# Gate and up projections: a second level of the seven-product scheme in six of ten weight slots, and one order of products

## The chip, the cores and the metric

The kernel runs on one core of one Trainium2 chip. The metric is device time in microseconds; the median of three runs of the kernel before is 2923.05 us.

## What is computed

The program is two different two-layer transformer stacks, one behind the other. The change lies in the feed-forward part of the second stack's two layers:

```python
def swiglu_ffn(u, w_gate_up, w_down):
    g, up = jnp.split(u @ w_gate_up, 2, axis=-1)
    return (jax.nn.silu(g) * up) @ w_down
```

`u` is 512 tokens by 1024 features, float32. `w_gate_up` has 2 x 2816 columns, `w_down` 2816 rows. What comes before it in each layer (mixing, attention over a memory) and the whole first stack with its experts are untouched.

## The kernel before

**Slots.** The gate and up weights come in 11 slots of 512 columns: two tiles of 128 gate columns and the two tiles of 128 up columns that belong to them, for all 1024 rows (2 MB). Two slots are in SBUF at a time; SyncE loads slot n + 2 when slot n has been read. Slot 0 is multiplied plainly. Slots 1 to 10 go by the Winograd form of Strassen's scheme: with the rows of the weights cut into a low and a high half, gate and up as the other cut, and the 512 tokens cut into two halves, the 2 x 2 by 2 x 2 block product is made with seven block products in place of eight.

**The seven products.** `a11`, `a12` are the low and high rows of gate, `a21`, `a22` those of up. VectorE forms `s1` to `s4` from them for every slot (`form_sums`, lines 2526 to 2531, four operations of 1024 columns) and `t1` to `t4` once a layer from the tokens. TensorE makes `P1 = a11 b11`, `P2 = a12 b21`, `P6 = s2 t2`, `P7 = s3 t3`, `P5 = s1 t1`, `P4 = a22 t4`, `P3 = s4 b22` (all products are issued at line 2551, `block_product`). A slot is worked as two chunks of 128 gate columns; each product is then four matmuls of 128 x 128 weights by 256 tokens, and each float32 matmul is two MATMUL records, each with a weight load. ScalarE copies P1, P7 and P5 from PSUM into small buffers (lines 3109 to 3112) and applies SiLU (3114, 3116), VectorE adds the others to them (3119, 3121, 3129, 3130) and multiplies gate by up (3133, 3136), and GpSimd makes the three sums that two corners share (3140, 3142, 3144). Each chunk uses four PSUM banks, the next one the other four.

**What sets the order.** Each engine runs its own fixed list; semaphores tie them together. Counters with the places of the steps in those lists say what to wait for (`g_full`, `g_act`, `g_dve`, `g_pool`, `g_sums`). VectorE forms the sums for the next slot in the middle of the second chunk's work. After the gate slots come eight slots of the down projection, which use the same scheme and the same banks.

Of the kernel before, what the change touches and what calls it, by code (L numbers as in the profile page):

```python
# [5 lines left out]
P = 128  # L6
# [73 lines left out]
def program(nc, a):  # L80
# [5 lines left out]
    with ctx:  # L86
# [2395 lines left out]
        quarters = [view(wk, i * 256, 256) for i in range(8)] + [view(rows, i * 256, 256) for i in range(4)]  # L2482
        feat_diff = [view(big, i * 1024, KC // 2, 256) for i in range(4)]
        w_sum = [[view(big, 4096 * (1 + b) + i * 1024, KC // 2, 256) for i in range(4)] for b in range(2)]
# [4 lines left out]
        FAST = {"mix": 10, "query": 2, "gate": FC - 2, "down": 4}  # L2489
        UP_FULL, SILU = {k: 7 for k in STAGES}, {"mix": 3, "query": 3, "gate": 5, "down": 5}  # L2490
        HIDDEN, ADDED = {"mix": 4, "query": 4, "gate": 6, "down": 4}, {k: 3 for k in STAGES}
        SUMS = {"mix": 6, "query": 2, "gate": FC // 2, "down": DOWN_SLOTS}

        def stage_base(per, halves, l, stage):
            each = [per[k] * FAST[k] // halves for k in STAGES]
            return l * sum(each) + sum(each[:STAGES.index(stage)])

        def g_full(stage, l, n, i):
            return LAYERS * PAIRS + stage_base(UP_FULL, 2, l, stage) + 7 * (n // 2) + 4 * (n % 2) + i + 1

        def g_act(stage, l, n, i):
            return LAYERS * PAIRS + stage_base(SILU, 1, l, stage) + SILU[stage] * n + i + 1

        def g_dve(stage, l, n, i):
            return LAYERS * PAIRS + stage_base(HIDDEN, 1, l, stage) + HIDDEN[stage] * n + i + 1

        def g_pool(stage, l, n, i):
            return stage_base(ADDED, 1, l, stage) + 3 * n + i + 1

        def g_sums(stage, l, b):  # L2510
            return l * sum(SUMS.values()) + sum(SUMS[k] for k in STAGES[:STAGES.index(stage)]) + b + 1

# [29 lines left out]

        def weight_sums(dve, n, w, b):

            dve.wait_ge(w_loaded[n % 2], 16 * (n // 2 + 1))
            sums(dve, w, w_sum[b % 2])
# [527 lines left out]
        P1_P2, P6_, P7_P5, P4_P3 = range(4)  # L3074
        P1_READ, P7_READ, P5_READ, LOW_SILU, HIGH_SILU = range(5)
        LOW_GATE, U2_READY, HIGH_GATE, LOW_UP, LOW_DONE, HIGH_DONE = range(6)
        U3_READY, HIGH_UP, U4_READY = range(3)

        def fast_chunk(name, eng, l, k, w, block_end, after_u2=None):

            b, i = divmod(k, 2)
            n = k - 2
            cols = slice(i * P, (i + 1) * P)
            p1_, p7_, p5_, u2, low, high = quarters[6 * (n % 2):6 * (n % 2) + 6]
            first, second = split_banks(fast_banks[l][n % 2])
            if name == "pe":
                gate, up = w[:, :, cols], w[:, :, 256 + i * P:256 + (i + 1) * P]
                s1, s2, s3, s4 = (v[:, :, cols] for v in w_sum[b % 2])
                t1, t2, t3, t4 = feat_diff
                lo, hi = LOW_K, HIGH_K  # L3090

                if k >= 4:
                    eng.wait_ge(hidden_ready, g_dve("gate", l, n - 2, LOW_UP))
# [8 lines left out]
            if name == "act":  # L3102
                if k == 2:
                    eng.wait_ge(bank_read_dve, reads_of[up_at[l, 1]]["dve"])
                if n >= 2:
                    eng.wait_ge(outer_added, g_pool("gate", l, n - 2, U4_READY))
                    eng.wait_ge(hidden_ready, g_dve("gate", l, n - 2, HIGH_DONE))
                eng.wait_ge(up_full, g_full("gate", l, n, P1_P2))
                A.activation(p1_, first[0], ACT.Copy).then_inc(silu_ready, 1)
                eng.wait_ge(up_full, g_full("gate", l, n, P7_P5))  # L3110
                A.activation(p7_, first[2], ACT.Copy).then_inc(silu_ready, 1)
                A.activation(p5_, second[2], ACT.Copy).then_inc(silu_ready, 1)
                eng.wait_ge(hidden_ready, g_dve("gate", l, n, LOW_GATE))
                A.activation(low, low, ACT.Silu).then_inc(silu_ready, 1)
                eng.wait_ge(hidden_ready, g_dve("gate", l, n, HIGH_GATE))
                A.activation(high, high, ACT.Silu).then_inc(silu_ready, 1)
            if name == "dve":
                eng.wait_ge(silu_ready, g_act("gate", l, n, P1_READ))
                V.tensor_tensor(low, p1_, second[0], ALU.add).then_inc(hidden_ready, 1)
                eng.wait_ge(up_full, g_full("gate", l, n, P6_))  # L3120
                V.tensor_tensor(u2, p1_, first[1], ALU.add).then_inc(hidden_ready, 1)
                if after_u2 is not None:
                    after_u2()
                if i:
                    eng.wait_ge(bank_full, block_end + 1)
                else:
                    eng.wait_ge(up_full, g_full("gate", l, n, P4_P3))
                eng.wait_ge(outer_added, g_pool("gate", l, n, U4_READY))
                V.tensor_tensor(high, p5_, second[3], ALU.add).then_inc(hidden_ready, 1)
                V.tensor_tensor(hidden[:, k, LO], p7_, first[3], ALU.add).then_inc(hidden_ready, 1)  # L3130
                eng.wait_ge(silu_ready, g_act("gate", l, n, LOW_SILU))
                eng.drain()
                V.tensor_tensor(hidden[:, k, LO], hidden[:, k, LO], low, ALU.mult).then_inc(hidden_ready, 1)
                eng.wait_ge(outer_added, g_pool("gate", l, n, HIGH_UP))
                eng.wait_ge(silu_ready, g_act("gate", l, n, HIGH_SILU))
                V.tensor_tensor(hidden[:, k, HI], hidden[:, k, HI], high, ALU.mult).then_inc(hidden_ready, 1)
# [12 lines left out]
        def gate_up(name, eng, l):  # L3149
# [19 lines left out]
            for blk in range(FC // 2):  # L3169
                n = take(name, "ring")  # L3170
                w = ring_slot(n, KC, 512)
                if name == "pe":
                    eng.wait_ge(w_loaded[n % 2], 16 * (n // 2 + 1))
                if name == "pe" and blk == 0:
                    first, second, banks = slice(0, 2 * P), slice(2 * P, 4 * P), []
                    feat_ready(eng, 1)
                    for i in range(2):
# [4 lines left out]
                        if i == 0:  # L3182
                            turn_x(name, eng, TT - 1)
# [653 lines left out]
```

## Time and profile before

| | us |
|---|---|
| median of three runs (2922.53 to 2923.17) | 2923.05 |
| span of the profiled execution | 2921.3 |
| TensorE busy, of the span | 2810.8 |
| VectorE busy | 1110.9 |
| ScalarE busy | 663.0 |
| GpSimd busy | 512.2 |

The busy time of an engine is the union of its records. Matmul records overlap, since a matmul is pipelined behind the one before it; the distance between their starts is what one costs in a long row of them. PE is TensorE, PEld its weight loads, DVE VectorE, ACT ScalarE, POOL GpSimd. An operation on VectorE that has no `drain` before it starts a little before the end of the one ahead; after a `drain` it starts a little behind that end.

### The profile page before, as it was taken

What the parts mean: (1) busy time and instruction counts of PE and PEld (TensorE: products, weight loads), DVE (VectorE), ACT (ScalarE), POOL (GpSimd) and SP (SyncE); (2) the same over time, 40 slices, a digit from 0 to 9 for tenths busy, and PEclk for the clock granted to TensorE, in tenths of its full rate; (3) what the DMA queues carried; (4) which work ended last, traced back from release to release, by engine and by line L of the source; (5) the groups of instructions that cost most, each with busy time, mean ns of one, the idle gap of its engine ahead of it and who ended that gap; (6) DMA issues with size and microseconds to landing.
All of it is one profiled execution on the core that took longest, in us unless ns stands there. A gap on an engine that the chain in (4) does not pass through costs nothing.

```text
span 2921.3 us, 32166 instructions
## 1 busy us (share of the span) xinstructions
PE 2810.8 (96%) x12444; PEld 1896.7 (65%) x12444; DVE 1110.9 (38%) x2252; ACT 663.0 (23%) x1512; POOL 512.2 (18%) x785
## 2 busy tenths in 40 slices
PE   8999999899999998999999999999999999999998
PEld 4565543355656432686565688888686575788887
DVE  4543311154433111445432333354446332333354
ACT  3333110033331100105422211101206412211100
POOL 3101111131111111113200022201114410122201
PEclk9999999999999999999999999999999999999999
DMA  3206799831067998420020222222220111122222
GB/s 135 75 29 252 292 425 423 363 127 56 30 259 305 424 425 359 175 87 30 30 87 29 87 87 87 72 80 94 87 87 30 49 67 47 69 87 87 72 90 84
DMA packets 106579, 422.13 MB, mean 145 GB/s; under 512 B 10096, under 2 KB 14320, under 8 KB 91440
## 3 DMA queue, kind: packets, MB, share of 16 engines
q1 hardware_dynamic: 93104, 387.01, 34.1%
q0 software_dynamic: 12736, 30.84, 2.8%
q8 instruction: 104, 1.70, 0.2%
q10 hardware_dynamic: 576, 2.10, 0.2%
q14 instruction: 59, 0.48, 0.1%
HBM read 408.63 MB, written 27.26 MB: 149 GB/s over the span
## 4 chain that ended last, share of the span: by engine, by line
PE 77%; issue 9%; DMA 7%; DVE 2%; ACT 2%; POOL 1%; POOLq 1%; DVEq 0%; SPq 0%; ACTq 0%
PE ps L2551 35%; PE ps L1773 6%; DMA ring_feat<-in_w 5%; PE ps L431 5%; PE ps L2792 4%; PE ps L2819 4%; PE ps L1112 3%; PE ps L1814 3%; PE ps L2693 2%; PE ps L2839 2%; PE ps L3153 2%; PE ps L1339 2%; PE ps L2283 1%; PE ps L2070 1%; PE ps L2265 1%
## 5 line engine op out<-in xcount | busy, mean ns | idle before, releaser
L431 PE MATMUL ps<-ring_feat 128*128 128x512 f32 (+2 forms) x704 | 274.9, 545 | 4.9 <-DMA ring_feat<-in_w_lat 2.8
L2551 PE MATMUL ps<-ring_feat 128*128 128x256 f32 x1216 | 277.0, 379 | 1.6 <-ACT big L287 1.6
L2551 PE MATMUL ps<-big 128*128 128x256 f32 x1200 | 268.1, 379 | 0.0
L2551 PEld LDWEIGHTS ps<-ring_feat 128*128 128x128 f32 x1216 | 230.9, 190 | 34.5 <-issue 3.3
L2551 PEld LDWEIGHTS ps<-big 128*128 128x128 f32 x1200 | 228.0, 190 | 31.0
L431 PEld LDWEIGHTS ps<-ring_feat 128*128 128x128 f32 x704 | 132.7, 191 | 130.6 <-issue 93.6
L2551 PE MATMUL ps<-tmp 128*128 128x256 f32 x576 | 128.6, 379 | 0.0
L2551 PE MATMUL ps<-ring_feat,tmp 128*128 128x256 f32 x544 | 126.6, 379 | 0.0
L2551 PEld LDWEIGHTS ps<-tmp 128*128 128x128 f32 x576 | 109.3, 190 | 14.8
L2792 PE MATMUL ps<-ring_feat 128*128 128x512 f32 x256 | 113.9, 596 | 5.0 <-ACT ring_feat L3052 2.7
L1112 PE MATMUL ps<-ring_feat 128*128 128x512 f32 x256 | 113.7, 595 | 0.0
L2551 PEld LDWEIGHTS ps<-ring_feat,tmp 128*128 128x128 f32 x544 | 103.3, 190 | 14.1
L2819 PE MATMUL ps<-ring_feat 128*128 128x512 f32 x256 | 111.8, 592 | 0.0
L1789 DVE TENSOR_TENSOR tmp<-tmp,ps 128x256 f32<-128x256 f32 x32 | 13.5, 421 | 247.7 <-ACT tmp L1783 247.7
L1828 POOL DMA_INDIRECT expert_out<-tmp,route_i x32 | 32.1, 1004 | 405.1 <-ACT tmp L1823 393.7
L1773 PE MATMUL ps<-big,tmp 128*64 128x512 f32 x416 | 93.4, 596 | 6.4 <-DVE tmp L1757 4.7
L2551 PE MATMUL ps<-ring_feat,big 128*128 128x256 f32 x400 | 95.5, 379 | 0.0
L2775 DVE TENSOR_TENSOR big<-ps,par 128x512 f32<-128x512 f32 x32 | 22.1, 692 | 185.3 <-ACT big L2771 185.3
L1757 DVE TENSOR_TENSOR tmp<-ps,par 128x512 f32<-128x512 f32 x64 | 41.2, 686 | 133.8 <-PE ps L1748 133.8
L1773 PE MATMUL ps<-ring_feat,tmp 128*64 128x512 f32 x384 | 86.0, 596 | 3.1 <-DVE tmp L1757 2.3
L2792 PEld LDWEIGHTS ps<-ring_feat 128*128 128x128 f32 x256 | 47.4, 190 | 63.8 <-issue 56.9
L2819 PEld LDWEIGHTS ps<-ring_feat 128*128 128x128 f32 x256 | 48.0, 190 | 57.4 <-issue 57.4
(501 smaller groups left out, 4663.8 us busy)
## 6 DMA issues: line engine op xcount, KB each, us to landing
big<-in_w SPq DMA_DIRECT2D x36, 2048.0 KB, 20.8
ring_feat<-in_w SPq DMA_DIRECT2D x36, 2048.0 KB, 27.7
ring_feat<-in_w_gate_up SPq DMA_DIRECT2D x22, 2048.0 KB, 8.0
ring_feat<-in_w_mix_in SPq DMA_DIRECT2D x12, 2048.0 KB, 8.1
e_spare<-in_w SPq DMA_DIRECT2D x12, 1792.0 KB, 25.7
par<-in_w SPq DMA_DIRECT2D x12, 1536.0 KB, 23.6
ring_feat<-in_w_down SPq DMA_DIRECT2D x12, 1536.0 KB, 6.7
tmp<-in_w_mem_kv SPq DMA_DIRECT2D x6, 2048.0 KB, 25.2
```

Of the source, the lines that this page charges most:

```text
L431: yield T.matmul(bank, lhs(k), rhs(k), start=k == 0, stop=k == n - 1)
L1112: m = T.matmul(bank, featv[:, k, t * P:(t + 1) * P], w[:, k, :], start=k == 6, stop=k == 2)
L1339: m = T.matmul(bank_of(q)[:, 0:N_MEM], w[:, k, i * P:(i + 1) * P], memT[:, k, :], start=k == 0, stop=k == KC - 1)
L1757: m = V.tensor_tensor(e_xT[p % 2][:, 4 * b:4 * b + 4, :], ps[:, b, :].rearrange("p (k s) -> p k s", k=4), g[:, 4 * b:4 * b + 4].unsqueeze( ...
L1773: m = T.matmul(ps[h, u, :], e_xT[s][:, k, h], e_half(l, c, i)[k % 4], start=k == 0, stop=k == KC - 1)
L1814: m = T.matmul(ps[h, 6 + half, :], e_hT[:, k, h], e_half(l, c, i)[2 * k + half], start=k == 0, stop=k == 1)
L2551: m = T.matmul(to, lhs[:, j, :], rhs[:, j, :], start=start and j == 0, stop=stop and j == chunks - 1)
L2693: yield T.matmul(bank, featv[:, k, t * P:(t + 1) * P], w[:, k, :], start=k == 0, stop=k == KC - 1)
L2792: m = T.matmul(begun["banks"][t], featv[:, k, t * P:(t + 1) * P], begun["w"][:, k, :], start=k == 0, stop=k == KC - 1)
L2819: yield T.matmul(bank, featv[:, k, t * P:(t + 1) * P], w[:, k, :], start=k == 0, stop=k == KC - 1)
L2839: m = T.matmul(bank[:, tokens], w[:, k, (f % 4) * P:(f % 4 + 1) * P], featv[:, k, tokens], start=k == 0, stop=k == KC - 1)
L3153: m = T.matmul(bank[:, tokens], w[:, kk, o:o + P], featv[:, kk, tokens], start=kk == 0, stop=kk == KC - 1)
```

## The change

Slots 2, 3, 5, 6, 8 and 9 get a second level: inside each of the seven products the scheme is applied again, so that a product is seven inner products of half the rows, 128 columns and 128 tokens. An inner product is two matmuls for each of its blocks, with 128 tokens in place of 256. For that each of the seven left operands needs its own four inner sums, each 128 partitions by 256 columns: VectorE forms them for six of the operands in each of these slots (`form_left`, which is a `drain` and then `form_sums`), GpSimd for the seventh, `a22` (`weight_sums`). The inner sums of the tokens' operands are made once a layer, in slots 0 and 1: two by VectorE (`form_right`), five by GpSimd (`token_sums`).

All slots, also those with one level, change their order. The two chunks are worked together: a product is made for the whole slot (512 PSUM columns with one level; 7 x 128 = 896 with two), in the order P1, P6, P7, P5, P2, P4, P3, and the products take four pairs of banks in turn. The results stay in one buffer `corner` of four parts, 512 or 896 columns wide; ScalarE's copies and the additions on VectorE and GpSimd span that width. With two levels the seven inner results of each of the four corners are then put together by GpSimd: `corners`, seven additions of 256 columns for the low tokens and seven for the high ones, before SiLU and the multiplication. `form_slot` makes the outer sums `s3`, `s2`, `s1`, `s4` one by one (1024 columns each), at four places of VectorE's list. Inner sums live in buffers that are unused at that time and in blocks of the slot itself that have been read.

TensorE's waits come to be one or two for every product: for the operand's sums, and for the reader of the product that used its pair of banks four products ago. The last slot's multiplications move behind the sums of down slot 1, and down slot 3 waits for them. The diff, cut to its core:

```diff
-        FAST = {"mix": 10, "query": 2, "gate": FC - 2, "down": 4}
...
-                block_product(first[0], gate[:, lo, :], featv[:, lo, LO])
-                block_product(second[0], gate[:, hi, :], featv[:, hi, LO]).then_inc(up_full, 1)
-                eng.wait_ge(blocks_summed, g_sums("gate", l, b))
-                block_product(first[1], s2, t2).then_inc(up_full, 1)
-                block_product(first[2], s3, t3)
-                block_product(second[2], s1, t1).then_inc(up_full, 1)
-                block_product(first[3], up[:, hi, :], t4)
-                block_product(second[3], s4, featv[:, hi, HI]).then_inc(bank_full if i else up_full, 1)
...
+        SLOTS_UP = range(1, FC // 2)
+        TWO_LEVEL = (2, 3, 5, 6, 8, 9)
+        PRODUCTS = ("P1", "P6", "P7", "P5", "P2", "P4", "P3")
+        LEFT = dict(P1="a11", P6="s2", P7="s3", P5="s1", P2="a12", P4="a22", P3="s4")
+        RIGHT = dict(P1="b11", P6="t2", P7="t3", P5="t1", P2="b21", P4="t4", P3="b22")
+        SEVEN = 7 * P
+        s_block = {f"s{i + 1}": view(big, 4096 + i * 1024, KC // 2, 256) for i in range(4)}
...
+                y11, y12, y21, y22 = right_parts(tok)
+                s1, s2, s3, s4 = left_sums(l, w, LEFT[p])
+                t1, t2, t3, t4 = right_sums(l, tok)
+                for q, (lhs, rhs) in enumerate(((part(x, X11), y11), (part(x, X12), y21), (s4, y22), (part(x, X22), t4),
+                                                (s1, t1), (s2, t2), (s3, t3))):
+                    m = block_product(to[:, q * P:(q + 1) * P], lhs, rhs, 2)
+                return m
...
+                n, p = 1 + i // 7, PRODUCTS[i % 7]
+                if p in ("P1", "P7", "P5"):
+                    pe.wait_ge(*copied(l, p.lower(), n))
...
+                    pe.wait_ge(*added(l, dict(P6="u2", P2="c11", P4="c21", P3="c12")[p], n))
...
+                    op, tok = LEFT[p], RIGHT[p]
+                    if p == "P1":
+                        ring_n = slot_w["pe", n][0]
+                        pe.wait_ge(w_loaded[ring_n % 2], 16 * (ring_n // 2 + 1))
+                    if two and op == "a22":
+                        pe.wait_ge(*outer(l, op, n))
+                    elif two or op[0] == "s":
+                        pe.wait_ge(*formed(l, op, n))
+                    if p == "P4":
+                        pe.wait_ge(*formed(l, "s4", n))
+                    if n == TWO_LEVEL[0] and tok in TOKENS_AT:
+                        pe.wait_ge(*tokens(l, tok))
+                    space_free(p, n)
+                    product(p, n).then_inc(bank_full if p == "P4" else up_full, 1)
...
+                if n > 1:
+                    act.wait_ge(*added(l, "low", n - 1))
+                copy("P1", C11, n)
+                if n > 1:
+                    silu(C12, n - 1)
+                copy("P7", C21, n)
+                if n > 1:
+                    act.wait_ge(*added(l, "high", n - 1))
+                copy("P5", C22, n)
+                silu(C11, n)
...
+            dve.drain()
+            form_sums(dve, *[part(x, b) for b in (X11, X12, X21, X22)], left_sums(l, w, op)).then_inc(blocks_summed, 1)
...
+            for n in SLOTS_UP:
+                two_now, two_next = n in TWO_LEVEL, n + 1 in TWO_LEVEL
+                if n > 1:
+                    last_corner(n - 1)
+                form_slot(dve, l, n)[3]()
+                if n > 1:
+                    multiply(0, n - 1)
+                if two_now:
+                    form_left(dve, l, "s4", n)
+                if n > 1:
+                    multiply(1, n - 1)
+                if n == 1:
+                    form_right(dve, l, "b11")
+                    form_right(dve, l, "t2")
+                dve.wait_ge(*full(l, "P6", n))
+                dve.wait_ge(*copied(l, "p1", n))
+                dve.drain()
+                V.tensor_tensor(corner[:, C12, 0:width_of(n)], product_space(l, "P6", n), corner[:, C11, 0:width_of(n)],
+                                ALU.add).then_inc(hidden_ready, 1)
+                if n < LAST_UP:
+                    third, second, first, fourth = form_slot(dve, l, n + 1)
+                    third()
+                    second()
+                    if two_next:
+                        dve.wait_ge(*full(l, "P1", n))
+                        form_left(dve, l, "a11", n + 1)
+                        form_left(dve, l, "s2", n + 1)
+                        form_left(dve, l, "s3", n + 1)
+                    first()
+                    if two_next:
+                        form_left(dve, l, "s1", n + 1)
+                else:
+                    dve.wait_ge(*full(l, "P7", n))
+                    down_sums(dve, l, 0, slot_w["dve", n][0] + 1)
+                add("P2", C11, n).then_inc(hidden_ready, 1)
+                dve.wait_ge(*outer(l, "c22", n))
+                add("P4", C21, n).then_inc(hidden_ready, 1)
+                if two_next:
+                    form_left(dve, l, "a12", n + 1)
+            last_corner(LAST_UP)
...
+            def corners(half, n):
+                pool.wait_ge(*added(l, ("c21", "c12")[half], n))
+                q = [in_halves[:, half, :, i * P:(i + 1) * P] for i in range(7)]
+
+                def add(to, more):
+                    return G.tensor_tensor(out=q[to], in0=q[to], in1=q[more], op=ALU.add)
+
+                add(5, 0)
+                add(1, 0)
+                pool.drain()
+                add(6, 5)
+                pool.drain()
+                add(5, 4)
+                add(3, 6)
+                pool.drain()
+                add(2, 5)
+                add(4, 6).then_inc(outer_added, 1)
...
+            for n in SLOTS_UP:
+                if n - 1 in TWO_LEVEL:
+                    corners(1, n - 1)
+                c12, c21, c22 = (corner[:, c, 0:width_of(n)] for c in (C12, C21, C22))
+                pool.wait_ge(*added(l, "u2", n))
+                pool.wait_ge(*copied(l, "p7", n))
+                G.tensor_tensor(out=c21, in0=c21, in1=c12, op=ALU.add).then_inc(outer_added, 1)
+                if n == 1:
+                    token_sums("t4")
+                pool.drain()
+                pool.wait_ge(*copied(l, "p5", n))
+                G.tensor_tensor(out=c12, in0=c12, in1=c22, op=ALU.add).then_inc(outer_added, 1)
+                pool.drain()
+                G.tensor_tensor(out=c22, in0=c22, in1=c21, op=ALU.add).then_inc(outer_added, 1)
+                if n + 1 in TWO_LEVEL:
+                    weight_sums(n + 1)
+                if n == 1:
+                    pool.wait_ge(bank_full, before_end)
+                    token_sums("t1")
+                    token_sums("b22")
+                if n in TWO_LEVEL:
+                    corners(0, n)
+            if LAST_UP in TWO_LEVEL:
+                corners(1, LAST_UP)
```

## Rows read from the trace of the kernel before

**Rows 1.** The page: busy us of the engines, share of the span, instructions.

```profile
PE 2810.8 (96%) x12444; PEld 1896.7 (65%) x12444; DVE 1110.9 (38%) x2252; ACT 663.0 (23%) x1512; POOL 512.2 (18%) x785
```

**Rows 2.** The chain of waits, in order of time: start us, us, what.

```profile
1671.90 363.05 PE ps L2551 x1682
```

**Rows 3.** Windows (last columns: granted clock, DMA): gate slots, then a stretch waiting for weights.

```profile
1672.00:1914.00 242.00, 242.00 (x1123) 213.00 (x1122) 94.58 (x162) 34.81 (x99) 50.38 (x60) 1.00 0.24 83
2537.00:2779.00 242.00, 242.00 (x1123) 213.00 (x1122) 94.59 (x163) 34.82 (x100) 50.38 (x60) 1.00 0.24 83
...
1062.00:1103.00 41.00, 32.84 (x152) 12.43 (x154) 6.40 (x12) 3.84 (x5) 6.08 (x6) 1.00 1.01 424
```

**Rows 4.** Groups by form, 1672 to 1914, VectorE: shapes, count | busy, mean ns.

```profile
L2526 DVE TENSOR_TENSOR big<-ring_feat 128x1024 f32<-128x1024 f32 x9 | 11.0, 1218 | 0.0
L3121 DVE TENSOR_TENSOR cst<-cst,ps 128x256 f32<-128x256 f32 x10 | 4.2, 421 | 8.1 <-PE ps L2551 8.1
L3167 DVE TENSOR_TENSOR tmp<-cst,ps 128x512 f32<-128x512 f32 x1 | 0.7, 689 | 6.2 <-PE ps L3153 6.2
```

**Rows 5.** Timeline of VectorE (start us, us): steps without and with a drain.

```profile
1689.54 1.22 DVE L2526 TENSOR_TENSOR big<-ring_feat 128x1024 f32<-128x1024 f32 x1
1690.68 1.22 DVE L2527 TENSOR_TENSOR big<-ring_feat 128x1024 f32<-128x1024 f32 x1
1691.97 1.23 DVE L2529 TENSOR_TENSOR big<-big,ring_feat 128x1024 f32<-128x1024 f32 x1
...
1696.77 0.42 DVE L3129 TENSOR_TENSOR rows<-rows,ps 128x256 f32<-128x256 f32 x1 [2.27 <-POOL rows L3144]
1697.11 0.41 DVE L3130 TENSOR_TENSOR tmp<-cst,ps 128x256 f32<-128x256 f32 x1
1697.62 0.43 DVE L3133 TENSOR_TENSOR tmp<-tmp,rows 128x256 f32<-128x256 f32 x1
```

**Rows 6.** Groups by form, GpSimd, whole span.

```profile
L3140 POOL TENSOR_TENSOR cst<-cst 128x256 f32<-128x256 f32 x20 | 14.5, 727 | 227.0 <-ACT cst L3112 217.8 <-ACT cst L3114 9.2
...
L473 POOL TENSOR_TENSOR krope<-krope,rope 128x16 f32<-128x16 f32 x32 | 6.1, 221 | 1.1
...
L989 POOL TENSOR_TENSOR par<-par,cst 128x512 f32<-128x512 f32 x2 | 2.2, 1092 | 0.0
```

**Rows 7.** Timeline of GpSimd: additions with a drain between them.

```profile
1682.26 0.73 POOL L3142 TENSOR_TENSOR tmp<-cst 128x256 f32<-128x256 f32 x1 [0.16 <-issue]
```

**Rows 8.** Timeline of VectorE at 1911: two additions of two SBUF operands, 512 columns.

```profile
1911.20 1.00 DVE L2519 TENSOR_TENSOR big<-ring_feat,big 128x512 f32<-128x512 f32 x1
1912.28 0.97 DVE L2521 TENSOR_TENSOR big<-ring_feat,big 128x512 f32<-128x512 f32 x1
```

**Rows 9.** Timeline of GpSimd in the same stretch.

```profile
1911.02 0.64 POOL L3140 TENSOR_TENSOR cst<-cst,rows 128x256 f32<-128x256 f32 x1 [9.59 <-ACT rows L3112]
1911.81 0.89 POOL L3142 TENSOR_TENSOR tmp<-cst,rows 128x256 f32<-128x256 f32 x1 [0.16 <-issue]
1912.86 0.97 POOL L3144 TENSOR_TENSOR rows<-rows 128x256 f32<-128x256 f32 x1 [0.16 <-issue]
```

**Rows 10.** Groups by form, 1672 to 1914: the same VectorE shape by itself.

```profile
L2531 DVE TENSOR_TENSOR big<-tmp,big 128x512 f32<-128x512 f32 x1 | 0.7, 693 | 0.1
```

**Rows 11.** Timeline of TensorE, start us, us: narrow matmuls in a row.

```profile
808.07 2.44 PE L823 MATMUL ps<-big,tmp 128*128 128x97 f32 x20
810.35 1.70 PE L740 MATMUL ps<-big,cst 128*128 128x64 f32 x14
```

**Rows 12.** One line, L2283, 2240 to 2242: duration ns min/median/max; 128 columns.

```profile
L2283 PEld LDWEIGHTS ps<-big,tmp x8: 186/192/192, 2240.6 to 2241.4; 128*128 128x128 f32 x8
L2283 PE MATMUL ps<-big,tmp x8: 275/275/377, 2240.6 to 2241.5; 128*128 128x128 f32 x8
```

**Rows 13.** ScalarE by form, whole span: 512 columns from SBUF to SBUF.

```profile
L3328 ACT ACTIVATE par<-big 128x512 f32<-128x512 f32 x16 | 10.1, 629 | 20.1 <-DVE big L3345 19.2
```

**Rows 14.** DMA issues: KB each, median us to landing.

```profile
ring_feat<-in_w_gate_up SPq DMA_DIRECT2D x22, 2048.0 KB, 8.0
```

More of the change, by code:

```diff
@@ new lines, in program, with part, spare_piece @@
+        corner = view(big, 8192, 4, SEVEN)
+        C11, C12, C21, C22 = range(4)
+        in_halves = corner.rearrange("p (r h) n -> p h r n", h=2)
+        def part(v, block):
+            return v[:, block[0], block[1]]
+        def spare_piece(l, i):
+            for buf, first, n in ((e_spare, 0, 14), (rows, 0, 6), (cst, P, 14), (par[l], PAR2["mix_post"][0], 8),
+                                  (par[l], PAR2["sub_g"][0], 1), (big, 11776, 2)):
+                if i < n:
+                    return view(buf, first + i * 256, 2, P)
+                i -= n
@@ new lines, in left_block, with left_sums @@
+        def left_block(w, op):
+            if op in s_block:
+                return s_block[op]
+            return w[:, LOW_K if op == "a11" else HIGH_K, HI if op == "a22" else LO]
+        def left_sums(l, w, op):
+            unused = w[:, LOW_K, HI]
+            if op == "a22":
+                return [part(unused, b) for b in (X11, X12, X21)] + [part(left_block(w, op), X21)]
+            at = {"a11": 24, "s2": 27, "s3": 31, "a12": 34, "s1": 37, "s4": 40}[op]
+            fourth = {"s2": spare_piece(l, 30), "a12": part(unused, X22)}.get(op)
+            return [spare_piece(l, at + i) for i in range(3)] + [part(left_block(w, op), X21) if fourth is None else fourth]
@@ new lines, in gate_up @@
+            n = take(name, "ring")
+            w = ring_slot(n, KC, 512)
+            if name == "pe":
+                eng.wait_ge(w_loaded[n % 2], 16 * (n // 2 + 1))
+                first, second, banks = slice(0, 2 * P), slice(2 * P, 4 * P), []
+                feat_ready(eng, 1)
+                for i in range(2):
+                    for o, reader in ((i * P, "act"), (256 + i * P, "dve")):
+                        banks.append((open_bank(eng, reader), o))
+                        up_at[l, i] = count[("pe", "bank")] - 1
+                        products(banks[-1][0], w, o, first)
+                    if i == 0:
+                        turn_x(name, eng, TT - 1)
+                feat_ready(eng, 3)
+                for bank, o in banks:
+                    products(bank, w, o, second).then_inc(bank_full, 1)
+                    take(name, "full")
+                used = [where[q] for q in range(count[("pe", "bank")] - 8, count[("pe", "bank")])]
+                fast_banks[l] = [used[0:4], used[4:8]]
+                slot_done(name)
+                up_pe(eng, l)
+                return
@@ new lines, in gate_up @@
+            at = []
+            for i in range(2):
+                at.append(take(name, "bank", 2))
+                if i == 0:
+                    turn_x(name, eng, TT - 1)
+            first_full = take(name, "full", 4)
+            if name == "dve":
+                eng.drain()
+                differences(eng, featv, feat_diff)
+                up_entry(eng, l)
+            if name in ("act", "dve"):
+                for i in range(2):
+                    silu(i, at[i], first_full + 2 * i)
+                    multiply(i, at[i], at[i] + 1, first_full + 2 * i + 1)
@@ L3444, in down_projection @@
             j0 = 0 if nxt is None else take(name, "norm", TT)
[L3445 to L3446 removed]
+            sets = fast_banks[l]
             ends = []
```

350 lines of the change are left out of this document (218 added, 132 removed).

## The prediction, made before the changed kernel was run

> **What bounds the kernel now.** I read the page first: TensorE is busy 96% of the span, the next engine 38% [rows 1]. Then the chain of waits: from 1671.90 it is one piece, 1682 records of line 2551 in 363.05 us, so 0.2158 us for a record of 256 columns [rows 2]. Then the windows: each layer's ten gate slots last 242 us, TensorE has no gap in them at full granted clock, VectorE works 94.6 us, GpSimd 50.4 [rows 3]. A slot has 2 chunks x 28 matmuls x 2 records = 112 records or 24.2 us, ten have 241.7. Whatever is taken from TensorE here is gained, as long as VectorE and GpSimd keep up; the question is what they get to do.
>
> The profiled execution's only figure is its span, 2921.3; the median is 1.75 above it. Differences below are put on the median.
>
> **TensorE's part.** A slot with two levels has 7 x 7 inner products of 2 matmuls for 2 column tiles: 98 matmuls, 196 records of 128 columns. Rows of narrow records: 20 of 97 columns in 2.44 us and 14 of 64 in 1.70; without the last one's 0.275 that is 0.114 and 0.110 a step, the same for both widths, so the weight load sets it [rows 11, 12]. At 0.112 the slot takes 21.95 us. Six of those and four of 24.17 are 228.4: 13.3 us saved a layer, 26.6 in all. That is about the most the change can give. The ends of this term: 0.108 (half of 0.2158) and 0.114, which make 223.7 and 230.8.
>
> **VectorE's list.** An operation of n columns lasts 0.421 us for 256, 0.689 for 512, 1.22 for 1024, so about 1.09 for 896 [rows 4]. The next one starts 0.08 before its end, or 0.08 behind it after a drain [rows 5]. One `form_left` is four operations of 256, three of them behind a drain: 0.34 + 3 x 0.50 = 1.84. For a slot with two levels: six `form_left` 11.0, four blocks of 1024 4.9, four additions of 896 4.2, two multiplications 1.2: 21.3 us. With one level 4.9 + 2.6 + 1.2 = 8.7. A period of three slots (two levels twice, one level once) has 51.3 of TensorE's 68.0. Alone, VectorE would fit.
>
> **GpSimd's list.** An addition of 256 columns lasts 0.727, one of 16 0.221, one of 512 with operands in two tensors 1.092 [rows 6]; a drain adds 0.16 [rows 7]. At 2.1 ns a column one of 896 takes 2.07 and one of 512 1.27; the ends for 896 are 1.86 (the slope from L3142's 0.64 [rows 9] to 1.092) and 2.54 (3.5 times 0.727). Two levels: 14 additions for the corners, 4 for `a22`, 3 of 896, ten drains: 13.1 + 6.2 + 1.6 = 20.9 us. One level 4.1. Three slots: 45.9 of 68.0. Alone it would fit too.
>
> **They are not alone.** At 1911.02 an addition on GpSimd starts and ends at 1911.66. A VectorE addition with both operands in SBUF starts at 1911.20 and takes 1.00 us, where the same shape takes 0.693 by itself [rows 8, 10]: its own work began 0.15 before GpSimd's end. The next GpSimd addition starts at 1911.81 and takes 0.89 in place of 0.64: it began 0.14 before VectorE's end. Then VectorE 0.97, then GpSimd 0.97 for 0.73 [rows 8, 9]. So the two take turns, each waits for whoever came first, and a hand-over gives back about 0.15. In the slots before, little met: 60 short operations of GpSimd in 242 us [rows 3]. Now nearly all of both lists is of this kind. Per period, by duration: VectorE two-SBUF work is 24 x 0.42 + 4 x 1.22 + 2 x 0.69 = 16.3 for two levels, 6.3 for one, 38.9 in all; GpSimd 19.3, 19.3 and 3.8, 42.4 in all. Together 81.3 us, more than TensorE's 68.0. Additions with one operand in PSUM are not counted.
>
> The Trainium skill, SBUF — State Buffer, "Who interferes with whom", has the shared pair held for the full instruction by whoever starts first, the other fully blocked. The rows have the turns, but the second starts 0.15 early. By the page nothing is given back and the period below would be 94 us, not 84.
>
> **The loop that closes through both.** The order of the lists makes a ring from the end of `c21` of one two-level slot (n = 3) to the same of slot 6:
> - A. GpSimd's 14 corner additions, 14 x 0.73 + 6 x 0.16 = 11.2; SiLU 0.63 [rows 13] and hand-overs 0.3; VectorE's block `s4` and one multiplication take turns in it, 1.9: 14.0. VectorE then stands at `multiply(1)`, and everything behind that waits: `u2` of slot 4, by which TensorE's P4 gets its banks.
> - B. VectorE from there to `c21` of slot 5: 0.6 + 0.8 (`u2`), blocks 2.4, three `form_left` 5.5, block 1.1, one 1.8, two additions 1.2, `a12` 1.8, 0.6, block 1.3, multiply 0.6, `s4` 1.8, multiply 0.6, `u2` 1.2, then 2.4 + 5.5 + 1.1 + 1.8 + 2.0: 34.1. GpSimd's work that takes turns in it: 3.8 + 6.2 (three additions each of slots 4 and 5) and twice 2.9 (`a22`): 15.8. Sum 49.9.
> - C. As A for slot 5, with `a12`, block, multiply and `s4` in it (5.3), and `u2` of slot 6: 11.2 + 0.9 + 5.3 + 1.8 = 19.2.
> - D. GpSimd's three additions of 896 for slot 6 (6.5), three blocks of VectorE in turns (3.7), `c21` 1.0: 11.2.
>
> Sum 94.3. In it are 45 operations of GpSimd; each has one or two hand-overs, at one and a half of 0.15 they give back 10. Period 84 us. Bounds: without any turn-taking A to D are 67.6, and TensorE's 68.0 sets it; with nothing given back 94. I take 84: it lies just above the 81.3 that the pair has to carry, as it must.
>
> **The sum.** Slot 1 has one level and its operands ready: 24.2. Slots 2 to 10 are three periods: 24.2 + 3 x 84 = 276.2 against 241.7, which is 34.5 us a layer and 69.0 for two: 2923.05 + 69 = 2992.
>
> Costed at nothing: the tokens' inner sums (five on GpSimd, 3.2 each), since GpSimd has nothing else in slot 0 and three additions in slot 1; if that cover is gone slot 2 loses up to one of them, 3. The weights: asked for behind P4 of slot n - 1, landed 8.0 later [rows 14], first read by VectorE behind P6 of slot n, 9.4 us of TensorE later; when the slots stretch the margin grows. The entry to the down slots: down slot 0 needs `c12` of slot 10 only for its second half, 6 us on, and the multiplications moved behind down slot 1's sums are wanted at down slot 3; if VectorE is later than 6 us, the surplus adds. ScalarE works 34.8 us in ten slots now [rows 3]; its copies widen by three quarters at most, and it stays under a quarter busy; what delays it is VectorE's multiplications.
>
> **Rivals.**
> 1. TensorE stays the bound: the turns are finer for 256-column operations than rows 8 and 9 show, or most of GpSimd's additions fall beside VectorE's PSUM additions. For it: each list alone fits, 51.3 and 45.9 of 68.0. Against it: 81.3 us of exclusive work. A period of 70 gives 234.2, 15 us less in all: 2908. The two sides part at a period of (241.7 - 24.2) / 3 = 72.5 us.
> 2. Nothing is given back in the short operations, period 94.3: 307.1 a layer, 3054. For it: three of four operations of VectorE stand behind a drain, so a waiting GpSimd gets in every time. Against it: all four hand-overs of rows 8 and 9 gave 0.14 or more.
> 3. The narrow records get slower in rows of 196. The longest rows in the trace are 20 and 14 [rows 11]. At 0.15 a record three slots are 83.0 and TensorE only meets the other bound. The far end is a load that nothing overlaps, 0.192 [rows 12]: the period is 99.4, and 3085.
>    The Trainium skill, TensorE: Matmul & The Clock Gate, "Back-to-back issue gap", gives 81 ns a matmul sustained at 128 columns against 56 for one alone. An estimate from that page's ratio, 0.112 x 81/56 = 0.162, makes the period 87.7, and 3014; the rows so far show the lower price.
> 4. TensorE, idle a fifth of the time, loses its clock. The trace has 41 us with TensorE busy 32.8 at a granted 1.00 [rows 3], the same share. If half of the records ran at half clock, a period had 34 us more of TensorE work, 102 in all, and with VectorE's waits stretched perhaps 105: 339 a layer, 3118.
>
> **Numbers.** Forecast (period 79 to 90) 0.77; rival 1 0.08; rival 2 0.06; rival 3 0.03; rival 4 0.02; a period between 72.5 and 79 0.04. Two tenths of a per cent, 5.8 us, is what a measurement tells from nothing. Faster 0.07, same 0.03, slower 0.90. The range takes the forecast's ends and a little of both neighbours: period 79 is 261.2 and 2962, 90 is 294.2 and 3028. I put 2960 to 3028.
>
> **What would show it.** In the gate windows after: 270 us or more for slots 1 to 10, TensorE's gaps ended by VectorE (lines of `u2`, `c11` and `form_left`), VectorE's 256-column operations at a mean well over 0.42 and GpSimd's well over 0.73, narrow records 0.112 apart, clock 1.00. It would be wrong if VectorE's mean stays at 0.42 with GpSimd busy, or if TensorE is busy throughout.

## The result, and the profile after

The changed kernel takes 2993.68 us (median of 4 runs, 2989.83 to 2995.91), the kernel before in the same session 2922.89 (4 runs). The ratio is 1.0238, with a 95% interval of 1.0223 to 1.0252: slower, and 1.7 us from the 2992.0 predicted. The profiled run took 2993.05, of which the span is 2991.3.

The page's first part, beside [rows 1]: TensorE has hardly more busy time though it has less to do, VectorE 243 us more, GpSimd 247.

```profile
PE 2816.9 (94%) x13452; PEld 1932.6 (65%) x13452; DVE 1353.6 (45%) x2436; ACT 662.5 (22%) x1412; POOL 759.5 (25%) x981
```

The windows of both gate stages (columns as in [rows 3]: TensorE, its weight loads, VectorE, ScalarE, GpSimd, granted clock, DMA).

```profile
1675.80:1951.00 275.20, 244.61 (x1627) 230.45 (x1626) 216.95 (x257) 34.39 (x49) 166.28 (x150) 0.94 0.23 79
2573.90:2848.00 274.10, 244.07 (x1626) 229.84 (x1624) 216.25 (x256) 34.39 (x49) 165.54 (x150) 0.94 0.22 79
```

Ten slots take 274.9 and 274.2 us, from the first record of slot 1 to the first of the down slots, where they took 241.7. TensorE stands idle for 30.6 and 30.0 of them. The two stages are 65.6 of the 70.0 us by which the span grew; 3.9 lie ahead of the first gate stage (last section), 0.4 behind it.

What TensorE waits for in the first stage (total us, times, longest):

```profile
PE ps L2545 <- DVE big L3339: 19.4, 6, 4.4
PE ps L2545 <- DVE big L3369: 5.8, 4, 2.3
PE ps L2545 <- ACT big L3251: 2.7, 2, 2.2
PE ps L2545 <- issue: 2.7, 2, 2.1
```

L3339 is `add` (`c11`, `c21` and `last_corner`), L3369 is `u2`, L3251 the copies: all gaps but 2.7 us are waits for PSUM banks that somebody must read out. The results lie ready in the banks; the readers stand behind other work in their lists. The largest gaps are in front of P6 of slots 3, 5, 6, 8 and 9 (17.0 us of the 19.4): P6 takes the banks of P2 of the slot before, and `c11`, which reads that P2, comes behind `u2`, the blocks and four `form_left` in VectorE's list. The 2.7 us are 2.08 in front of P1 of slot 3, where the inner sums of `a11` come late, and 0.60 in front of P5 of slot 2, where GpSimd's `t1` sums of the tokens do.

Why that work takes so long is in the groups by form of the stage (count | busy, mean ns | idle before, ended by), beside [rows 4] and [rows 6]:

```profile
L3296 DVE TENSOR_TENSOR big<-ring_feat,big 128x1024 f32<-128x1024 f32 x9 | 24.0, 2671 | 0.7
L3339 DVE TENSOR_TENSOR big<-ps,big 128x896 f32<-128x896 f32 x18 | 19.0, 1082 | 2.9 <-POOL big L3457 2.9
L3349 DVE TENSOR_TENSOR tmp<-big 128x512 f32<-128x512 f32 x18 | 16.6, 925 | 38.6 <-ACT big L3259 38.6
L2526 DVE TENSOR_TENSOR cst<-ring_feat 128x256 f32<-128x256 f32 x6 | 10.9, 1812 | 0.0
...
L2528 DVE TENSOR_TENSOR cst<-cst,big 128x256 f32<-128x256 f32 x12 | 5.1, 426 | 0.9
...
L3427 POOL TENSOR_TENSOR big<-big 128x256 f32<-128x256 f32 x84 | 68.3, 834 | 8.7 <-DVE big L3339 3.6
L3450 POOL TENSOR_TENSOR big<-big 128x896 f32<-128x896 f32 x6 | 17.6, 2939 | 24.8 <-DVE big L3369 17.1 <-ACT big L3251 7.7
```

The same VectorE operation of 256 columns has a mean of 1.81 us at one place of the list and 0.43 at another; 1024 columns with both operands in SBUF have 2.67 for 1.22. The addition that reads PSUM, 896 wide, has 1.08 everywhere. GpSimd's 896 columns have 2.94, and its corner additions 0.83 for 0.73.

Six lines of the timelines of the two engines, one stretch (start us, us), show the turns:

```profile
1799.67 2.95 DVE L3296 TENSOR_TENSOR big<-ring_feat,big 128x1024 f32<-128x1024 f32 x1
1802.70 2.15 DVE L2525 TENSOR_TENSOR cst<-ring_feat 128x256 f32<-128x256 f32 x1
1804.77 2.31 DVE L2526 TENSOR_TENSOR cst<-ring_feat 128x256 f32<-128x256 f32 x1
```

```profile
1798.55 2.99 POOL L3450 TENSOR_TENSOR big<-big 128x896 f32<-128x896 f32 x1 [7.37 <-DVE big L3369]
1801.70 2.86 POOL L3455 TENSOR_TENSOR big<-big 128x896 f32<-128x896 f32 x1 [0.16 <-issue]
1804.72 2.08 POOL L3457 TENSOR_TENSOR big<-big 128x896 f32<-128x896 f32 x1 [0.16 <-issue]
```

GpSimd's 2.86 ends at 1804.56. VectorE's operation of 0.42, issued at 1802.70, ends at 1804.85, so its own work began at 1804.43, 0.13 before that end. GpSimd's next one, issued at 1804.72, takes its bare 2.08 and ends at 1806.80; VectorE's second 0.42 ends at 1807.08 and began at 1806.66. An operation of 0.42 took 2.31 us, and no gap shows in VectorE's row: waiting for the pair counts as busy.

The same place of the list stands in the chain of waits once in each of the three periods (slots 2, 5 and 8), 83.38 and 83.40 us apart. The view calls these 8.00 us "issue"; GpSimd's timeline gives them as a wait of 8.03 for VectorE's sums of `s1`:

```profile
1723.42 8.00 issue
...
1806.80 8.00 issue
...
1890.20 8.00 issue
```

```profile
1814.83 0.73 POOL L3415 TENSOR_TENSOR ring_feat<-ring_feat 128x256 f32<-128x256 f32 x1 [8.03 <-DVE big L2530]
```

### The profile page after: what moved, and what is told of

The parts are those of the page before. It is cut to its first block, busy times and chain, and to the rows that moved or that the text cites. A ratio compares the mean times of both kernels' runs of the same rounds, so it can differ in the third digit from the quotient of the medians.

```text
span 2991.3 us, 34838 instructions
## 1 busy us (share of the span) xinstructions
PE 2816.9 (94%) x13452; PEld 1932.6 (65%) x13452; DVE 1353.6 (45%) x2436; ACT 662.5 (22%) x1412; POOL 759.5 (25%) x981
## 4 chain that ended last, share of the span: by engine, by line
PE 58%; issue 14%; POOL 7%; DMA 7%; POOLq 7%; DVE 4%; ACT 2%; DVEq 1%; SPq 0%; ACTq 0%
PE ps L2545 20%; PE ps L1773 5%; DMA ring_feat<-in_w 5%; PE ps L431 5%; PE ps L1112 4%; PE ps L2813 3%; PE ps L2786 3%; PE ps L1814 3%; POOL big L3427 2%; PE ps L2687 2%; PE ps L2833 2%; PE ps L3476 2%; PE ps L1339 2%; POOLq L3453 1%; POOLq L3456 1%
## 5 line engine op out<-in xcount | busy, mean ns | idle before, releaser
L431 PE MATMUL ps<-ring_feat 128*128 128x512 f32 (+2 forms) x704 | 274.9, 545 | 5.0 <-DMA ring_feat<-in_w_lat 2.9
L2545 PE MATMUL ps<-ring_feat 128*128 128x256 f32 (+1 forms) x1168 | 233.4, 351 | 11.1 <-ACT big L3251 5.4
L2545 PE MATMUL ps<-big 128*128 128x256 f32 (+1 forms) x1008 | 195.1, 350 | 34.6 <-DVE big L3339 33.4
L2545 PEld LDWEIGHTS ps<-ring_feat 128*128 128x128 f32 x1168 | 198.4, 192 | 35.1 <-issue 13.8
L431 PEld LDWEIGHTS ps<-ring_feat 128*128 128x128 f32 x704 | 132.7, 191 | 130.7 <-issue 93.6
L2545 PEld LDWEIGHTS ps<-big 128*128 128x128 f32 x1008 | 170.4, 199 | 52.7 <-issue 22.5
L3427 POOL TENSOR_TENSOR big<-big 128x256 f32<-128x256 f32 x168 | 136.6, 834 | 17.5 <-DVE big L3339 7.2
L3259 ACT ACTIVATE big<-big 128x512 f32<-128x512 f32 x40 | 25.2, 629 | 385.7 <-POOL big L3427 283.3
L2545 PE MATMUL ps<-ring_feat,big 128*128 128x128 f32 (+1 forms) x496 | 90.2, 327 | 0.0
```

Of the source, the lines that this page charges most:

```text
L431: yield T.matmul(bank, lhs(k), rhs(k), start=k == 0, stop=k == n - 1)
L2545: m = T.matmul(to, lhs[:, j, :], rhs[:, j, :], start=start and j == 0, stop=stop and j == chunks - 1)
L3427: return G.tensor_tensor(out=q[to], in0=q[to], in1=q[more], op=ALU.add)
```

## Experiments

Each kernel was timed beside the kernel before, on the same chip. For e1_order, e6_floor, e3_oneinput and e4_allone that kernel's median was 2924.11 us (13 runs), for the other four 2925.79 (21 runs). A difference between kernels of different groups is uncertain by the 1 to 3 us by which that kernel's medians differ. All start from the changed kernel.

**e1_order: the new order alone.**

```
-        TWO_LEVEL = (2, 3, 5, 6, 8, 9)
+        TWO_LEVEL = ()
```

> No slot has a second level; the new order of products, the common buffer of 512 columns and the tokens' inner sums stay. Theory (turn-taking between VectorE and GpSimd, made by the second level's additions): slots 1 to 10 take 241.7 us as before, TensorE has no gap, 2923 +- 3. Rival (the new order itself makes TensorE wait): a period of three slots stays near 83 us or at least above 73, and the time stays above 2940.

Measured: 2925.53 us (2921.04 to 2930.43, 10 runs), ratio 1.0002 (0.9992 to 1.0012). The stage is 241.73 us in both layers, without a gap, the same as before to the hundredth. What the change costs, it costs through the second level.

**e6_floor: TensorE's part alone.** All of TensorE's products stay, of VectorE's and GpSimd's inner work a quarter or less: one of the four inner sums is made and used for all four, and one of seven corner additions.

```
-                s1, s2, s3, s4 = left_sums(l, w, LEFT[p])
+                s1 = s2 = s3 = s4 = left_sums(l, w, LEFT[p])[3]
...
-            form_sums(dve, *[part(x, b) for b in (X11, X12, X21, X22)], left_sums(l, w, op)).then_inc(blocks_summed, 1)
+            s1, s2, s3, s4 = left_sums(l, w, op)
+            V.tensor_tensor(s4, part(x, X12), part(x, X22), ALU.subtract).then_inc(blocks_summed, 1)
```

> TensorE's work is that of the changed kernel, but the second level's own additions are left out: of each operand's four inner sums one is made (VectorE's and GpSimd's), it is used for all four, and of the seven corner additions one stays. Theory: TensorE alone sets the pace, 6 x 21.95 + 4 x 24.17 = 228.4 us for slots 1 to 10, total 2896 (2893 to 2901), narrow records 0.112 us apart over rows of 196. Rival (narrow matmuls are dear in long rows): at 0.162 a record 287 us and 3014.

Measured: 2899.06 us (2895.66 to 2904.02, 4 runs), ratio 0.9918 (0.9902 to 0.9935). The stage is 228.01 us in both layers; its window:

```profile
1671.90:1899.70 227.80, 227.80 (x1625) 216.25 (x1624) 160.12 (x147) 34.64 (x49) 82.71 (x60) 1.00 0.26 91
```

Busy throughout, and 0.112 us a record in rows of 196: (228.01 - 4 x 24.17) / 6 = 21.9 a slot.

**e3_oneinput and e4_allone: the same lists without the shared operand.** If the pair is held only by VectorE operations with two operands in SBUF, an operation with one, of the same length, leaves it free. In e3 the four operations of `form_left` become reductions over an axis of one element, in e4 the blocks of 1024 too. Counts, lengths, waits and GpSimd's list stay; what is stored is a copy of one operand, not the sum, so the outputs differ.

```
+            def one(to, x):
+                return V.tensor_reduce(to, x.unsqueeze(3), AX.X, ALU.add)
+            one(s1, a21)
+            one(s3, a11)
+            dve.drain()
+            one(s2, s1)
+            dve.drain()
+            one(s4, a12).then_inc(blocks_summed, 1)
```

```
-                m = V.tensor_tensor(s_block[op], x, y, how)
+                m = V.tensor_reduce(s_block[op], x.unsqueeze(3), AX.X, ALU.add)
```

> VectorE's inner sums (six operands of four operations in every slot with two levels) become operations of one SBUF input, a reduction over an axis of one element, with the same count, width, drains and waits; their values are not the sums, so this part of the computation is changed. GpSimd's work is untouched. Theory: these 48 operations of a period stop taking turns with GpSimd, whose additions then meet only the blocks of 1024 and the multiplications. Exclusive work falls from 81.3 to 61.1 us a period; ring B loses its 5.8 for a22 and C about 3.4, give-backs aside, so the period is 76 to 79, slots 1 to 10 about 256 us, total 2957 (2948 to 2966). Rival (the ring of waits is long by itself, whatever the port does): nothing changes, 2993.

> As the one before, and VectorE's outer sums (four blocks of 1024 columns a slot) are reductions of one input too, same widths; the sums are not formed. Only the two multiplications a slot still take both operands from SBUF. Theory: the ring falls to its length without turns, 67.6, TensorE's 68.0 sets the pace but for single short waits; slots 1 to 10 take 229 to 234 us, total 2898 to 2908, faster than the kernel before the change although no engine has less to do. Rival (lists and waits alone): 2993. Rival (narrow matmuls are dear): above 2960.

Measured: e3 2942.64 us (2940.48 to 2947.53, 4 runs), ratio 1.0066 (1.0049 to 1.0083); stages 249.3 and 248.6. e4 2902.28 us (2899.58 to 2907.68, 4 runs), ratio 0.9921 (0.9904 to 0.9937); stages 229.9 and 229.2. Groups by form of e4:

```profile
L3306 DVE TENSOR_REDUCE big<-ring_feat 128x1024 f32<-128x1024 f32 x27 | 32.5, 1213 | 5.5 <-PE ps L2545 4.8
L3437 POOL TENSOR_TENSOR big<-big 128x256 f32<-128x256 f32 x84 | 60.8, 744 | 8.7 <-DVE big L3349 3.6
L3460 POOL TENSOR_TENSOR big<-big 128x896 f32<-128x896 f32 x6 | 12.5, 2090 | 23.9 <-DVE big L3379 20.6 <-ACT big L3251 3.3
```

Blocks and GpSimd's additions are back at what they take alone, 1.21, 0.74 and 2.09 us, and with that the whole loss is gone and most of TensorE's gain appears. This is the experiment that shows the cause: the same number, length and order of operations in every list, only the two multiplications a slot left with two operands in SBUF, 91 us less. e3 has its direction right and its size wrong: 51 us came back where 36 were expected. Taking 48 short operations (20.2 us) out of a period's 81.3 leaves 61.1 of exclusive work, below TensorE, and the period fell to (249.3 - 24.2) / 3 = 75.0. In the middle period of the changed kernel these 48 last 29.9 us where their bare length is 20.2, so they wait 9.7 us for the pair (the 2.15 and 2.31 above are two of them), and 8.4 us of the period went with them; 5 to 8 had been expected. Which part of the ring gave up the rest was not followed.

The Trainium skill, SBUF — State Buffer, "Who interferes with whom", says the same of trn2: two SBUF inputs contend with a GpSimd instruction that reads SBUF, one does not, and a `tensor_reduce` never does. These runs agree, by the 1213 and 744 ns.

**e5_nocorner: relief on the other side.** Of `corners` only one line of the seven additions stays.

```
-                add(5, 0)
-                add(1, 0)
...
-                pool.drain()
-                add(2, 5)
                 add(4, 6).then_inc(outer_added, 1)
```

> The changed kernel with six of the seven additions of GpSimd left out in each half of the corners of a two-level slot (12 of 14 per slot; the inner products are not put together, so the output differs). VectorE's and TensorE's lists stay whole. Theory: 24 additions of 0.73 us and 14 drains of 0.16, 19.8 us, leave GpSimd's 45.9 a period, and exclusive work falls from 81.3 to 81.3 - 17.5 = 63.8, under TensorE's 68.0. VectorE still waits for GpSimd's additions of 896 and the four sums: worked through with the rows' durations the stage is 242.6 us a layer in place of 274.5, so some 14 us of gaps a layer are left: 2925, range 2915 to 2935, a gain of some 64 to 69 over the changed kernel. Rival (VectorE's own list is the bound once the ring is opened, GpSimd matters little): a gain under 30, 2965 or more. Rival (nothing is left of the ring): 228.4 a layer, 2896.

Measured: 2936.10 us (2930.34 to 2941.97, 10 runs), ratio 1.0034 (1.0025 to 1.0044); stages 249.7 and 247.4. A gain of 57.6 with VectorE's list whole: VectorE's own length is not the bound. But 11 us less gain than expected. The window shows why:

```profile
1674.10:1923.70 249.60, 238.12 (x1625) 225.76 (x1624) 208.69 (x255) 34.42 (x49) 105.09 (x78) 0.96 0.24 83
```

TensorE's gaps are 11.5 us, fewer than the expected 14, but it is busy for 238.1 where e6_floor has 227.8, at a granted clock of 0.96. For 20.5 us of this stage and 13.7 of the second the granted clock was 0.5, the level of 1.2 GHz, and narrow records were 0.213 apart there in place of 0.112: 20.5 x (1 - 0.112 / 0.213) = 9.7 us, and 6.5. 228.0 + 11.5 + 9.7 = 249.2 and 228.0 + 12.4 + 6.5 = 246.9. I had counted the gaps and not what follows them. In this kernel TensorE is nearly the bound, so the clock shows in the time.

**e2_three, e2b_alt, e2c_pairs: how many such slots, and where.** Nothing is left out in these; only `TWO_LEVEL` differs: (3, 6, 9), (2, 4, 6, 8) and (2, 3, 6, 7). The last two have the same number of every operation.

> Two levels in slots 3, 6 and 9 only, one in every three. Theory (the shared pair of VectorE and GpSimd sets the period): three slots hold one list of 35.6 us of exclusive work (16.3 + 19.3) and two of 10.1 (6.3 + 3.8), 55.8 in all, under TensorE's 21.95 + 2 x 24.17 = 70.3. The ring from one two-level slot to the next has two one-level slots in between, and closes sooner than TensorE. So TensorE sets the time: 24.17 x 7 + 21.95 x 3 = 235.0 us a layer against 241.7, no gap of over 1 us, no half clock, 13.4 us less than the kernel before: 2909.5, range 2905 to 2916, faster by 0.3 to 0.6%. Rival (every slot with two levels costs a fixed price, whatever stands beside it): after lost 32.8 us a layer with six of them, so three lose 16.4: 2956. Rival (narrow records or the new order are what costs): 2923 or more.

> Two levels in slots 2, 4, 6 and 8, every other one. Theory: two slots have 45.7 us of exclusive work against TensorE's 46.1, so the pair is just full: a queue of waits in the ring makes it somewhat longer than TensorE's part. By the two lists worked through step by step with the durations of the rows and turns that give back 0.15, the stage is 243.5 us a layer where TensorE's records alone are 232.5: some 11 us of gaps a layer, 3.5 us more than before in two layers: 2926, range 2915 to 2936. Rival (only a full pair counts, no ring): 232.5 a layer, 2904. Rival (a fixed price for each such slot): four lose 21.9 a layer, 2967.

> Two levels in slots 2, 3, 6 and 7: the same number of each operation as with 2, 4, 6 and 8, only placed as neighbours. Theory (the ring: GpSimd's corner additions of one two-level slot hold VectorE's list, and with it the sums that the neighbour's first product reads): the pair of neighbours overruns as in the changed kernel, 84 us for three slots, and the fourth slot, with one level, takes a part of the surplus back: worked through step by step 256.0 us a layer, 12.5 more than the alternating one, which is 25 more in all: 2951, range 2940 to 2962. Rival (the sum of exclusive work over the stage counts, not its place): the same time as slots 2, 4, 6 and 8, within 5 us.

| kernel | stages, us | TensorE's gaps | median, us (runs) | ratio to before, 95% |
|---|---|---|---|---|
| e2_three | 234.9, 234.9 | 0, 0 | 2911.98 (5) | 0.9956 (0.9943 to 0.9970) |
| e2b_alt | 243.7, 242.1 | 6.9, 6.9 | 2928.88 (10) | 1.0010 (1.0001 to 1.0019) |
| e2c_pairs | 255.5, 255.8 | 14.3, 15.7 | 2953.76 (4) | 1.0092 (1.0076 to 1.0107) |

All three came within 3 us of what the turns gave (2909.5, 2926, 2951), and the stages within 1.5 us of 235.0, 243.5 and 256.0. A fixed price for each such slot would have put e2_three at 2956. Neighbours cost 24.9 us more than alternating slots, with the same instructions: the place counts, not the sum over the stage.

In the last two the totals agree better than what they are made of. e2b_alt has 6.9 us of gaps a stage where 11 were expected, but also 6.8 us at a granted clock of 0.5 in the first stage and 3.4 in the second. By 1 - 0.112 / 0.213 that costs 3.2 and 1.6 us, and 1.6 us is what the second stage is shorter. e2c_pairs has 13.7 us at 0.5 in each stage, so of its 24.9 us over e2b_alt some 16 are gaps and some 8 are clock.

The window of e2_three:

```profile
1672.50:1907.20 234.70, 234.70 (x1373) 214.47 (x1372) 157.61 (x183) 31.79 (x49) 113.21 (x96) 1.00 0.25 88
```

TensorE has no gap. GpSimd and VectorE still wait for each other there (VectorE's `s2` block has a mean of 2391 ns, GpSimd's additions of 896 up to 2887), only now it is hidden behind TensorE. This version beats both kernels: 13.8 us less than before, 0.44%, and some 82 less than the changed one.

## Why the prediction was right

**TensorE's term.** 21.95 us a slot and 228.4 a stage were predicted; e6_floor has 21.9 and 228.0. Rival 3 is out: the rows of 20 and 14 [rows 11] did tell the price of a row of 196.

**The lists.** The estimates for shapes that the trace before did not have, 1.09 for VectorE's 896 columns and 2.07 for GpSimd's, came out at 1.08 and, where nothing met them, 2.08. Nothing in the sum rested on an end of the range.

**Taking turns.** The 0.14 and 0.15 of [rows 8, 9] are 0.13 to 0.14 in every hand-over of the timeline above, with the short operations too. Rival 2 (nothing given back) is out. VectorE's additions that read PSUM, which the prediction left out of the pair's work, did stay out of it (1082 ns).

**The ring.** The middle period can be read off by its operations: `c21` of slot 3 ends at 1760.07, `multiply(1)` starts at 1772.63, `c21` of slot 5 ends at 1816.75, `u2` of slot 6 at 1833.21, its `c21` at 1843.46.

| part | without give-back, predicted | measured | difference |
|---|---|---|---|
| A | 14.0 | 12.6 | 1.4 |
| B | 49.9 | 44.1 | 5.8 |
| C | 19.2 | 16.5 | 2.7 |
| D | 11.2 | 10.2 | 1.0 |
| sum | 94.3 | 83.4 | 10.9 |

I had taken 10 off and had a period of 84; it is 83.4.

**Mis-sized: what the hand-overs give back.** The 10.9 us are not all hand-overs. Put each operation's own work at the end of its record, with its bare length (0.42, 0.69 and 1.22 on VectorE, 0.73, 1.27 and 2.08 on GpSimd): the own work of the two engines then overlaps at 46 places of the period, by 0.12 to 0.15 each, 6.4 us in all. I had 45 operations at one and a half hand-overs, 10. The other 4.5 are for the most part in B, where the two `a22` sums were charged 5.8. They made VectorE's operations only 1.0 longer: part of them ran beside VectorE's additions from PSUM, which do not take turns, and those for slot 6 started at 1814.83, 1.9 before B ended; in C they cost 1.4.

```profile
1787.87 1.28 DVE L3339 TENSOR_TENSOR big<-ps,big 128x512 f32<-128x512 f32 x2
1789.65 0.94 DVE L2526 TENSOR_TENSOR par<-ring_feat 128x256 f32<-128x256 f32 x1
1814.67 2.08 DVE L3339 TENSOR_TENSOR big<-ps,big 128x896 f32<-128x896 f32 x2
```

```profile
1788.04 0.72 POOL L3415 TENSOR_TENSOR ring_feat<-ring_feat 128x256 f32<-128x256 f32 x1 [8.04 <-DVE big L2530]
```

So one term was too large and a second effect, which the sum did not have, made up for it. Nor are the 81.3 us a floor for the period, as the prediction says: less 6.4 they are 75.0, for so long the pair is held in the 83.4 us, and in the other 8.4 it is free while the lists wait for each other.

The timeline of VectorE at the joint of A and B, where the in-order list stands before the multiplications:

```profile
1767.03 1.23 DVE L3349 TENSOR_TENSOR tmp<-big 128x512 f32<-128x512 f32 x1 [4.37 <-ACT big L3259]
1772.63 0.69 DVE L3349 TENSOR_TENSOR tmp<-big 128x512 f32<-128x512 f32 x1 [4.38 <-ACT big L3259]
1773.42 0.69 DVE L3369 TENSOR_TENSOR big<-ps,big 128x512 f32<-128x512 f32 x1
```

They wait for ScalarE's SiLU, and its timeline says for what that waits:

```profile
1766.37 0.63 ACT L3259 ACTIVATE big<-big 128x512 f32<-128x512 f32 x1 [16.76 <-POOL big L3427]
...
1771.97 0.63 ACT L3259 ACTIVATE big<-big 128x512 f32<-128x512 f32 x1 [3.09 <-POOL big L3427]
```

They are GpSimd's corners, 14 additions in 11.78 us from 1760.16 on. `u2` had its product since about 1764.8 (slot 4 starts at 1757.93, two products of 3.45) and stood behind both multiplications until 1773.42. The prediction had TensorE's P4 of slot 4 wait for it; that P4 starts at 1775.20 without a gap. What TensorE waits for is further down the same list: `c11` of slot 4 (1787.87 above), and P6 of slot 5 starts behind it at 1788.70, after a gap of 3.31. This is how more work on GpSimd reaches TensorE's banks. In slots 3, 6, 9 and 10 P4 does wait for `u2`, 5.8 us in all.

**The sum.** 24.2 + 3 x 84 = 276.2 was predicted, 274.9 and 274.2 measured. The stages gave 65.6 of the 69.0 us, and what they lacked came from 3.9 us ahead of the first one, which the sum did not have. The stages are 1.3 and 2.0 us off. The path, the turns and the direction were forecast; that they come so close is partly luck, by the two terms above that cancel, and that of the total by one more.

**What was costed at nothing.** Order, buffers and weights cost nothing in e1_order. Of the tokens' sums one, `t1`, made slot 2 wait 0.60 us, where up to 3 had been named. The entry to the down slots has a gap of 2.4 us, which is inside the 274.9; in the sum it stood as a surplus that might be added.

**Wrong: the clock.** "Clock 1.00" was among the things to be seen; it is 0.94. For 30.7 us of each stage it was 0.5. The rival had the direction and a much larger size, half of all records at half clock: it was 11% of the time. TensorE is busy for 244.6 and not 227.8, 16.8 us more, and yet the period is what it was worked out to be with no such loss. My reading is that the ring through VectorE and GpSimd set it, and that at full clock the gaps would have been longer by as much; no run has the ring without the half clock, so this is not shown. The 1.00 of [rows 3] did not tell it: TensorE's share of work there is 80%, here 89%, and it has gaps of up to 2.58 us (at 1087.39) with no half clock behind them.

Rival 1 (TensorE stays the bound) is out by 30 us of gaps a stage.

## What to carry to other kernels

- Before you move work to VectorE and GpSimd at once, add up by duration what VectorE does with two operands in SBUF and what GpSimd does with SBUF: both together have to fit under the bound, and each list fitting alone says nothing. That is needed and not enough: in e5_nocorner the sum was 63.8 of 68.0 and 11.5 us of gaps a stage were left. Operations with an operand in PSUM, or with one operand, are not in that sum.
- Then follow the ring, that is, the loop of waits through lists that each run in order and wait for each other once per slot: it costs by place. Spread over the slots, the same instructions cost 25 us less, and half as many cost nothing and left a gain of 13.8.
- When an idle TensorE is part of a forecast, count what follows a gap too, and ask whether TensorE or somebody else is the bound there: in e5_nocorner it cost 16 us in two stages, more than the 11 missing from the gain, since the gaps were 4 shorter than expected. In the changed kernel it seems hidden.

## What the runs showed of the hardware

**Short gaps cost clock.** Windows of the changed kernel: a gap of TensorE, the stretch right behind it, and a stretch later.

```profile
1785.40:1788.70 3.30, 0.00 (x0) 0.03 (x1) 3.08 (x7) 0.11 (x1) 0.67 (x1) 1.00 0.22 82
1788.70:1792.00 3.30, 3.30 (x16) 3.30 (x17) 3.06 (x6) 0.52 (x1) 2.19 (x4) 0.52 0.00 0
1792.50:1797.00 4.50, 4.50 (x43) 4.50 (x42) 3.81 (x8) 1.58 (x3) 0.00 (x0) 1.00 0.03 5
```

TensorE did nothing for 3.3 us. The granted clock behind it is 0.52, the 1.2 GHz level for nearly all of it, and 16 records fill 3.3 us, 0.21 each; then 43 fill 4.5. Of the first stage's ten gaps of over 2 us, seven had such a stretch: 4.36, 2.29, 3.31, 3.45, 2.30, 3.40 and 2.17 us (ending at 1732.53, 1749.98, 1788.70, 1815.90, 1833.36, 1872.08 and 1911.08). Those of 2.08, 2.49 and 2.42 (1724.81, 1899.30, 1950.58) had none. In e1_order, e6_floor and e2_three, whose gate stages have no gap, the granted clock is 1.00 throughout them.

Length alone does not decide it. In e2b_alt the same gap comes in both layers, 1.97 us ending at 1849.26 and 1.99 ending at 2717.35; these are the windows behind them:

```profile
1849.30:1852.60 3.30, 3.30 (x16) 3.30 (x17) 3.06 (x6) 0.48 (x1) 2.15 (x4) 0.50 0.03 5
2717.40:2720.70 3.30, 3.30 (x30) 3.30 (x31) 3.06 (x6) 0.47 (x1) 2.15 (x4) 1.00 0.00 1
```

What tells a gap that has such a stretch from one that has none was not tried.

**It also moves between runs.** Ahead of the first gate stage both kernels are the same, and still the stage starts at 1671.74 in the profile before, 1675.68 in that after, 1680.22 in e4_allone's. A stretch of the changed kernel in which the kernel before had a granted clock of 1.00:

```profile
1340.80:1347.60 6.80, 5.22 (x24) 4.01 (x26) 4.71 (x14) 4.31 (x12) 4.23 (x7) 0.56 0.05 17
```

There, and around 1171 to 1181, 3.9 us are lost in this one execution. Single runs of the kernel before spread over 2921.8 to 2930.6 us; a difference of a few us between two profiles says nothing until the stage is named in which it arises.
